# Split-precision projections: two of three products become one matmul of 512 columns, and the halves of its bank are added at eviction

## The reference, cut to what matters

```python
hn = rms_norm(h, pre_norm_g[l])
proj = hn @ w_in[l]            # 256 x 2048 times 2048 x (thousands of columns)
...                            # mixer: sparse attention + RWKV, then differential attention, then gated linear attention
h = h + out @ w_out[l]         # 256 x 2048 times 2048 x 2048
```

## Time and profile before

| | |
|---|---|
| median of 3 runs | 1798.62 us (1797.42 to 1798.91) |
| span of the profiled execution | 1793.7 us |
| TensorE busy, records | 1719.0 us (96%), 13621 |
| VectorE busy | 1002.4 us (56%) |
| ScalarE busy | 788.1 us (44%) |
| mean granted TensorE clock | 0.981 |
| DMA | 254 MB, mean 142 GB/s |

### The profile page before, as it was taken

The page is one execution under the profiler, slowest core; times in us unless marked ns, Lnnn a source line. Parts: engine busy times, 40 slices in busy tenths (PEclk is TensorE's granted clock), DMA queues, the critical chain, the costliest instruction groups (busy, mean ns, idle before and its releaser), DMA issues. The chain is left out here.

```text
span 1793.7 us, 31345 instructions
## 1 busy us (share of the span) xinstructions
PE 1719.0 (96%) x13621; PEld 1639.8 (91%) x13621; DVE 1002.4 (56%) x1273; ACT 788.1 (44%) x1123; POOL 97.4 (5%) x88
## 2 busy tenths in 40 slices
PE   8999999899999898979999999999899999999899
PEld 7989998799998798978999989999898999999899
DVE  5665443664545265466454468887545854455443
ACT  6542223522222355444343348876436434444432
POOL 2210000300000000031000000000011000000000
PEclk9999999899999999989999999999999999999999
DMA  9643232433234915536666534444554655556363
GB/s 283 188 127 94 72 95 60 126 98 92 74 95 120 201 48 172 176 105 174 182 178 168 155 118 139 144 142 153 160 165 135 186 163 146 154 161 181 129 202 104
DMA packets 253584, 254.00 MB, mean 142 GB/s; under 512 B 9153, under 2 KB 249826, under 8 KB 253064
## 3 DMA queue, kind: packets, MB, share of 16 engines
q1 hardware_dynamic: 252792, 251.80, 47.9%
q0 software_dynamic: 656, 0.21, 0.1%
HBM read 249.29 MB, written 2.69 MB: 140 GB/s over the span
## 5 line engine op out<-in xcount | busy, mean ns | idle before, releaser
L213 DVE TENSOR_TENSOR w_lo<-w_raw,w_hi 128x1024 fp32r<-128x1024 f32 (+1 forms) x452 | 550.2, 1220 | 534.1 <-ACT w_hi L208 533.5
L241 PE MATMUL ps<-xt,w_hi 128*128 128x256 f32 x2736 | 805.8, 295 | 24.4 <-DVE w_lo L213 20.5
L242 PE MATMUL ps<-xt,w_hi 128*128 128x256 f32 x2736 | 779.7, 285 | 0.0
L243 PE MATMUL ps<-xt,w_lo 128*128 128x256 f32 x2736 | 779.2, 285 | 0.0
L208 ACT ACTIVATE w_hi<-w_raw 128x1024 fp32r<-128x1024 f32 (+1 forms) x452 | 470.2, 1045 | 667.1 <-PE ps L243 514.9
L241 PEld LDWEIGHTS ps<-xt,w_hi 128*128 128x128 f32 x2736 | 530.0, 194 | 49.5 <-issue 34.8
L242 PEld LDWEIGHTS ps<-xt,w_hi 128*128 128x128 f32 x2736 | 530.6, 194 | 1.2 <-issue 0.7
L243 PEld LDWEIGHTS ps<-xt,w_lo 128*128 128x128 f32 x2736 | 529.9, 194 | 0.0
L250 PE MATMUL ps<-w_hi,xt 128*128 128x256 f32 x832 | 244.0, 293 | 0.0
L251 PE MATMUL ps<-w_lo,xt 128*128 128x256 f32 x832 | 236.8, 285 | 0.0
L252 PE MATMUL ps<-w_hi,xt 128*128 128x256 f32 x832 | 236.6, 284 | 0.0
(11 more groups left out here) (395 smaller groups left out, 1531.4 us busy)
## 6 DMA issues: line engine op xcount, KB each, us to landing
w_raw<-in_a_w_in SPq DMA_DIRECT2D x128, 512.0 KB, 3.7
w_raw<-in_w_in SPq DMA_DIRECT2D x120, 512.0 KB, 3.6
w_raw<-in_b_w_in SPq DMA_DIRECT2D x96, 512.0 KB, 3.7
w_raw<-in_w_out SPq DMA_DIRECT2D x32, 512.0 KB, 4.2
w_raw<-in_a_w_out SPq DMA_DIRECT2D x32, 512.0 KB, 4.5
w_raw<-in_b_w_out SPq DMA_DIRECT2D x32, 512.0 KB, 3.5
arena<-in_x SPq DMA_DIRECT2D x4, 512.0 KB, 7.1
w_raw<-in_w_in SPq DMA_DIRECT2D x8, 256.0 KB, 3.8
```

The lines of the kernel that those rows point to most:

```text
L213: k.nc.vector.tensor_tensor(k.wl[:, p % RING, :, 0:w], k.raw[:, p % RAW, :, 0:w], k.wh[:, p % RING, :, 0:w].bitcast(F32), ALU.subtract).th ...
L241: pe.matmul(os, h[:, cs], xt[:, kt, 0:S], start=st and ct == 0, stop=False, skip_group_check=True)
L242: pe.matmul(os, h[:, cs], xt[:, kt, S:2 * S], start=False, stop=False, skip_group_check=True)
L243: last = pe.matmul(os, l[:, cs], xt[:, kt, 0:S], start=False, stop=sp, skip_group_check=True)
```

## The change

TensorE's part of the diff (the kind "tok" has the operands' roles exchanged: `both` is then the high and the low weights side by side, in a new joint tile `w_hilo`):

```diff
-G_BANK = 6
+G_BANK, G_BANKS = 5, 3
...
-                    pe.matmul(os, h[:, cs], xt[:, kt, 0:S], start=st and ct == 0, stop=False, skip_group_check=True)
-                    pe.matmul(os, h[:, cs], xt[:, kt, S:2 * S], start=False, stop=False, skip_group_check=True)
-                    last = pe.matmul(os, l[:, cs], xt[:, kt, 0:S], start=False, stop=sp, skip_group_check=True)
...
+        for u in range(nu):
+            o, unit = self.bank(c, u), self.unit(c, u)
+            if i % PIECES == 0 and unit >= G_BANKS:
+                pe.wait_ge(k.freed, unit - G_BANKS + 1)
+            for kk in range(KP):
+                if u or kk:
+                    yield
+                kt = (i % PIECES) * KP + kk
+                if spec["kind"] == "T":
+                    high = k.wx[:, p % RING, kk, 0, u * P:(u + 1) * P]
+                    both, low, single = xt[:, kt, :], k.wx[:, p % RING, kk, 1, u * P:(u + 1) * P], xt[:, kt, 0:S]
...
+                if kt < KT - 1:
+                    pe.matmul(o, high, both, start=kt == 0, stop=False, skip_group_check=True)
+                    mm = pe.matmul(o[:, S:2 * S], low, single, start=False, stop=False, skip_group_check=True)
```

An eviction now has to add the two halves of the bank. In the input projections and `out1`, ScalarE first copies the low half to a buffer in SBUF (`spill`), VectorE adds the high half (`summed`), and for kind "T" VectorE multiplies by the norm's scale in a third step (`scaled`). In `out2` and `out3` VectorE adds twice (`added_up`):

```diff
+def spill(k, g, act, c, u):
+
+    spec, n = g.chunks[c], g.unit(c, u)
+    g.done(act, c, u)
+    if n >= 2:
+        act.wait_ge(k.freed, n - 1)
+    out, low = k.low[:, n % 2, :], g.bank(c, u)[:, S:2 * S]
...
+def summed(k, g, dve, c, u):
+
+    spec, n = g.chunks[c], g.unit(c, u)
+    dve.wait_ge(k.spilled, n + 1)
...
+        k.nc.vector.tensor_tensor(spec["dst"][:, u, :], g.bank(c, u)[:, 0:S], k.low[:, n % 2, :],
+                                  ALU.add).then_inc(k.freed, 1)
...
+        k.nc.vector.tensor_tensor(spec["dst"][:, u, :], spec["dst"][:, u, :], k.rsb[:], ALU.mult).then_inc(k.evac_d, 1)
...
+def added_up(k, g, dve, c, u, out, other):
+
+    n = g.unit(c, u)
+    g.done(dve, c, u)
+    k.nc.vector.tensor_tensor(out, g.bank(c, u)[:, 0:S], other, ALU.add).then_inc(k.spilled, 1)
+    dve.wait_ge(k.spilled, n + 1)
+    k.nc.vector.tensor_tensor(out, g.bank(c, u)[:, S:2 * S], out, ALU.add).then_inc(k.freed, 1)
```

More of the change, by code:

```diff
@@ L176, in __init__, with count, unit, bank @@
         k.chunks += len(chunks)
-        self.starts, at = [], 0
+        self.starts, self.units, self.firsts, at = [], [], [], 0
         for c in chunks:
-            a, d = k.evacs[-1]
-            k.evacs.append((a + by_act(c), d + (not by_act(c))))
-            per = KP * (c["width"] // P if c["kind"] == "T" else NT)
+            nu = c["width"] // P if c["kind"] == "T" else NT
+            self.units.append(k.units)
+            self.firsts.append(k.firsts)
+            k.units += nu
+            k.firsts += nu - 1
+            k.evacs.append(k.evacs[-1] + nu * (inner and c["kind"] == "T"))
             for _ in range(PIECES):
                 self.starts.append(at)
-                at += per
+                at += KP * nu
         self.slots = at
-    def bank(self, c):
-        return self.k.ps[:, G_BANK + (self.c0 + c) % 2, :]
+    def count(self, c):
+        spec = self.chunks[c]
+        return spec["width"] // P if spec["kind"] == "T" else NT
+    def unit(self, c, u):
+        return self.units[c] + u
+    def bank(self, c, u):
+        return self.k.ps[:, G_BANK + self.unit(c, u) % G_BANKS, :]
     def load(self, e, upto):
@@ L259, in pe, with done, emptied @@
+        mm.then_inc(k.piece_used, 1)
+        yield
+    def done(self, e, c, u):
+        if u < self.count(c) - 1:
+            e.wait_ge(self.k.first_done, self.firsts[c] + 1)
+        else:
+            e.wait_ge(self.k.piece_used, self.p0 + PIECES * (c + 1))
+    def emptied(self, e, c):
+        e.wait_ge(self.k.freed, self.unit(c, self.count(c) - 1) + 1)
     def pe(self, pe):
@@ L281, in side @@
                 made += 1
-            end = self.starts[i + 1] if i + 1 < self.n else self.slots
-            for _ in range(end - self.starts[i]):
+            for step in range(KP * nu):
+                if step == KP and i % PIECES == PIECES - 1:
+                    end(c, 0)
                 yield
-        evac(len(self.chunks) - 1)
+        end(len(self.chunks) - 1, self.count(len(self.chunks) - 1) - 1)
 def merged(slots, stages, at, s0=0):
@@ L307, in drained @@
         pass
[L310 to L314, removed]
-    g.done(dve, c)
+def spill(k, g, act, c, u):
[4 more added lines that the diff above has]
+    out, low = k.low[:, n % 2, :], g.bank(c, u)[:, S:2 * S]
+    if spec["kind"] == "T":
+        k.nc.scalar.activation(out, low, ACT.Copy).then_inc(k.spilled, 1)
+    else:
+        k.nc.scalar.activation(out, low, ACT.Copy, scale=k.rst[:, u:u + 1]).then_inc(k.spilled, 1)
@@ L456, in turn @@
                 pe.wait_ge(self.pte, h)
+            else:
+                pe.wait_ge(self.te, 2)
             for br in range(2):
@@ L1548, in _, with scale @@
                 m.then_inc(dg, 1)
[L1550 removed]
+                def scale(c, u):
                     if c == 0:
@@ L2027, in _ @@
                 advance(steps, 4 * g1.slots // len(g1.chunks))
-                for n in range(5):
+                for n in range(4):
                     turn(n)
@@ L2394, in high @@
                                          scale=k.vb[:, B_N1 + kt:B_N1 + kt + 1]).then_inc(hd, 1)
-                drained(g1.act(act, lambda c: square(c - 1) if 0 < c < last else None, PIECES))
+                drained(g1.act(act, lambda c, u: square(c - 1) if u and 0 < c < last else None, PIECES))
                 for q in range(PIECES):
```

316 lines of the change are left out of this document (153 added, 163 removed).

## The result

The kernel after takes 1813.85 us (median of 4, 1812.82 to 1815.93) beside 1798.02 us of the kernel before: a ratio of 1.009, 95% interval 1.0072 to 1.0108. It is slower by 16 us, where 54 us less were forecast.

The account below looks back on a forecast made before the run. The prediction took TensorE's time per projection group as the bound. Span 1793.7 - 66 (groups) + 3 (differential attention) + 6 (waits) + 2 (ends) = 1738.7 us, plus 4.9 to the runs' median, gave 1744 us; range 1716 to 1807.

Parts of the forecast that it names:

- The bound: Whole kernel: TensorE busy 1719 of 1793.7 us; projection groups of three matmuls, 360 ns each, make 1284 us, 72% of the span.
- The price of the new group: Projections on TensorE: long matmul 221 ns plus short 120 gives 341 instead of 360, saving 66 us.
- second reading: Why 256 columns take 120 ns: a fixed cost of 13.3 ns per fp32r matmul, giving 227 ns for 512 columns.
- four readings: Explanations of 120 ns for 256 columns: weight load, fixed cost, limit on columns, or limit only where stream and load match.
- first reading: Why 256 columns take 120 ns: coupling with the weight load, which a stream of 512 columns would hide whole.
- Added work: Larger evictions: about 110 us more on VectorE and 75 on ScalarE, hidden where room; 3 us given back in differential attention.
- The new wait: TensorE needs a bank again after eight groups, 2.7 us, against 2.0 us of eviction work and split; 6 us for all waits.
- The ends and the lost bank: Longer chains at projection ends, 1.2 or 0.4 us each; lost bank, for transposes and sparse attention, nothing; together 2 us.
- The rival of columns: Each column costs 0.47 ns, so the long matmul takes 240 ns and nothing is saved: 1810 us, slower; chance 0.22.
- The rival of the new wait: TensorE waits for `freed` in most chunks beside mixers, costing 30 to 55 us: 1770 to 1795; chance 0.10.
- The rival in between: The long matmul takes 228 to 236 ns: 1765 to 1797 us; chance 0.08.
- What the profile would show: Right: starts 0.22 and 0.12 apart, `freed` waits under 10 us, attention chunks 14.4 us. Wrong: 0.24 and 0.12, or `freed` leading.

Follow-up runs that it names:

- experiment 2: Kernel before with its old banks and evictions, but one matmul of 512 columns and one of 256 per group (sums wrong, time only): 1770.32 us, ratio 0.9865.
- experiment 1: Probe computing nothing of the reference: series of 48 matmuls of several lengths and loads; 512 columns took 226.7 ns, 256 took 120.0, by turns 353.5 a pair.
- experiment 8: Kernel after, long-short order turned every second group: 1803.09 us; long always first: 1808.78 us. A probe of orders: ABAB 353.3 ns a pair, 343.3 with loads of 32 columns.
- mixed kernel: Three banks kept; 28 of 113 chunks back to three matmuls of 256 and one eviction, the others long-short and short-long by turns: 1778.52 us, ratio 0.9897.
- experiment 5: Kernel after with groups in pairs of pieces, so a bank is needed after 16 groups, not 8, and every second piece's split issued later: 1808.52 us, ratio 1.0072.
- second kernel of experiment 10: Like the mixed kernel, but the long matmul only in 23 of 24 output-projection chunks and five chunks where input projections begin: 1789.89 us, ratio 0.9966.
- experiment 3: Kernel after with its three banks, evictions and waits, but the matmul of 512 columns split into two of 256: 1832.87 us, ratio 1.0212.
- experiment 10: Two kernels with the old scheme in some chunks and the new in others, on the three banks: 1778.52 us (mixed kernel) and 1789.89 us.
- experiment 6: VectorE's scale of each unit cut to 8 of 256 columns (time only): on the kernel after ratio 1.0075, on the kernel of experiment 5 ratio 1.0032.
- turned groups: Long-short and short-long matmul order by turns, every second group turned; alone on the kernel after 1803.09 us, ratio 1.0037.

## Why the prediction was wrong

It gave 1744 (1716 to 1807) and 0.20 for slower. In the order of its steps:

- **The bound.** Right: TensorE's time for a group counts, and experiment 2 turned the new shape alone into 26 us.
- **The price of the new group: the step that failed first.** "I take 221 for the long one" and 120 for the short one, 341. A long matmul among its like costs 226.7 (experiment 1), the fixed cost that the prediction named as its second reading; that would be 347 for a group. In the kernel's own order it is 353.3 (236.7 and 116.7) in most places, because two lengths by turns cost 6.7 ns more than the sum of both. None of the four readings had the long matmul dearer beside short ones; the load has a part in it (experiment 8), but not the one of the first reading. The bounds of 216 to 240 held the 236.7 measured; the value between them was taken too low. 66 us of saving became about 24.
- **Added work.** 110 and 75 us forecast, 101 and 57 measured, at the prices of the rows; ScalarE's 75 was too much by its own price, since 155 spills of 0.383 are 59. That it was hidden "where a chunk has room" was true for most of the 85 wide chunks of the mixed kernel. In the differential attention 3 us were given back by forecast; there the loss is 7.4 us against before and 7.9 against experiment 2. VectorE, busy for 142.76 of 168.77 us, 85%, was not full; in seven of eleven chunks TensorE stood 0.5 to 1.5 us before the sum came, 6.9 us together.
- **The new wait: the step that failed second.** "I count 6 us for all such waits" against 30.1 us. The slack of 2.7 us was set against the operations of one eviction and one split (2.0 us). In the queues stood a mixer's whole step, six microseconds on VectorE at 1406.8, or on ScalarE a split whose weights had not arrived, 9.0 us of idle time before 600.46. The prediction named operations of 1.75 us beside mixers, but priced an average where the worst queue decides. That VectorE "is rarely behind" on average was of no help, and it left out ScalarE, whose spill comes first. Not all of the 30.1 us are loss (experiment 5).
- **The ends and the lost bank.** 2 us forecast. In the second kernel of experiment 10 the chunks around their ends (39 to 41, 80 to 83, 104 to 106) lose 2.0 + 2.1 + 0.2 = 4.3 us: right in kind. The lost bank was taken at nothing, and nothing was found (0.2 us over 85 chunks).
- **The rivals.** The rival of columns gave 1810 and 0.22, but its cause is not what happened: columns are not what costs. The rival of the new wait (30 to 55 us) had the mechanism and, with 37 to 40 us for banks and evictions, the size. How it was made up was otherwise: it counted on 0.5 to 1 us in half of the chunks, and 13 places waited, three of them for 21 us. The prediction let these rivals exclude each other. (The rival in between adds up to 1768 to 1796, not 1765 to 1797; nothing hangs on it.) In fact a smaller saving and a biting wait came together: 1796 - 26 + 40 = 1810. A sum of two moderate misses had no place in the chances or in the range.
- **What the profile would show.** It had named the signs: starts of 0.24 and 0.12, `freed` leading the waits, and chunks beside the attention over 14.7 us (168.77 / 11 = 15.3). All three came, but not for the causes named beside them: the starts were to mean that columns cost, and the long chunks that VectorE is full, and neither is so.

Shown by runs: the split into a gain of 22 to 26 and a loss of 37 to 40 us (experiments 2 and 3); that the loss needs the new evictions and not the lost bank, and sits in few places (experiment 10); that the deadline alone and the scale alone are not it (experiments 5 and 6). Only argued: that the clock has a share of it. Open: how much of the loss is ScalarE's queue and how much VectorE's, and the two rhythms.

## What to carry over

Price an eviction's deadline against the longest step or wait that can stand in front of it in the queue of each engine that it passes through, not against the engine's share or the eviction's own length; and where two unsure terms point the same way, give the case in which both go wrong a chance of its own. A change that gains in most places and loses in a few should be compared chunk by chunk: going back to the old scheme in a quarter of the chunks brought 25 us, and with the turned groups +16 us became -18. Before taking a price between bounds from relatives, remember that instructions of two lengths by turns can cost more than each among its like.

## What the runs showed of the hardware

- An fp32r matmul of N columns behind its like, with loads of 128 columns, takes N / 2.4 + 13.3 ns at full clock: 120.0 (256), 147 (320), 173.3 (384), 226.7 (512). 448 columns took 202.7, 2.7 more than that. Plain fp32 has 2 to 3 ns over its cycles: 215.8 and 429.1.
- With loads of 32 columns 256 columns fall to 113.1 ns and 512 rise to 232. A series of 128 columns takes 111.7, not the 66.7 of the sum, and close to the 113 ns at which loads of 128 columns follow each other in the earlier trace rows.
- 512 and 256 by turns take 353.3 ns a pair, 6.7 more than the sum; as ABBA or AABB 348.3. With loads of 32 columns the pair takes 343.3, and the extra is gone. In kernels the same ABAB also ran at 346.7 for whole chunks; six ways into the series in a probe gave 353.3 each time.
